# Two transformer blocks on one core: moving the second round of transposes behind the next scores on TensorE, in the attention of the first three layers

## What is computed

```python
def diff_attn(q, k, v, lam):
    s = jnp.einsum("bqhmd,bkhmd->bhmqk", q.astype(F32), k.astype(F32)) * (B_QK_DIM ** -0.5)
    p = jax.nn.softmax(s, axis=-1)
    a = p[:, :, 0] - lam * p[:, :, 1]
    return jnp.einsum("bhqk,bkhd->bqhd", a, v.astype(F32))
```

## Time and profile before

| | us |
|---|---|
| median of 3 runs | 4227.97 |
| lowest, highest | 4216.44, 4235.77 |
| the profiled execution | 4224.61 |
| its span, first to last instruction | 4222.8 |
| PE busy in it | 3709.6 (88%) |
| DVE busy | 1952.1 (46%) |
| ACT busy | 1164.9 (28%) |
| POOL busy | 401.1 (9%) |

### The profile page before, as it was taken

One profiled execution on the slowest core, in us unless ns is written; L12 is line 12 of the kernel. 1 busy time (PEld: TensorE's weight loads), 2 busy tenths in 40 slices (PEclk: granted clock), 3 DMA queues, 4 the chain that ended last, 5 costly groups with the idle time before them and its releaser, 6 DMA issues.

```text
span 4222.8 us, 50333 instructions
## 1 busy us (share of the span) xinstructions
PE 3709.6 (88%) x20543; PEld 2948.4 (70%) x20543; DVE 1952.1 (46%) x2990; ACT 1164.9 (28%) x1891; POOL 401.1 (9%) x340
## 2 busy tenths in 40 slices
PE   6987789999989778999898888899999679978996
PEld 4865577888878636777786546688888556657885
DVE  3443654424445364434322774542343544455454
ACT  3221422212222232222222552221121234433221
POOL 1030410000000031000000470000000013200000
PEclk8985999999999778999998999899999789989998
DMA  5430013323322101545411011232342111112331
GB/s 175 150 99 1 1 47 110 113 73 111 103 66 70 30 1 46 160 129 166 125 55 43 1 27 51 78 112 75 110 119 67 43 32 27 36 45 75 93 101 61
DMA packets 520933, 319.63 MB, mean 76 GB/s; under 512 B 51216, under 2 KB 512798, under 8 KB 520704
## 3 DMA queue, kind: packets, MB, share of 16 engines
q1 hardware_dynamic: 512160, 299.93, 24.5%
q0 software_dynamic: 8544, 16.47, 1.4%
HBM read 309.79 MB, written 4.55 MB: 74 GB/s over the span
## 4 chain that ended last, share of the span: by engine, by line
PE 83%; DVE 10%; ACT 4%; issue 3%; POOL 1%; DMA 0%; DVEq 0%; ACTq 0%; POOLq 0%
PE PS L878 79%; PE PS L1072 2%; DVE TMP L1782 1%; DVE HL L1765 1%; DVE ATT L1850 1%; DVE TMP L1718 1%; DVE TMP L1774 1%; DVE X L1725 1%; DVE X L2220 1%; ACT BIG L1456 1%; ACT SPH L1324 1%; DVE X L2223 0%; ACT TMP L1456 0%; DVE TMP L1799 0%; ACT TMP L1395 0%
## 5 line engine op out<-in xcount | busy, mean ns | idle before, releaser
L878 PE MATMUL PS<-HH,SPH 128*128 128x512 f32 (+1 forms) x3424 | 1193.7, 361 | 98.1 <-DVE HL L1765 68.8
L878 PE MATMUL PS<-HL,SPH 128*128 128x512 f32 (+1 forms) x3424 | 1167.0, 355 | 0.0
L878 PEld LDWEIGHTS PS<-HH,SPH 128*128 128x128 f32 x3424 | 654.6, 191 | 235.3 <-issue 78.9
L878 PE MATMUL PS<-HH,SPL 128*128 128x512 f32 (+1 forms) x3424 | 736.8, 353 | 0.0
L878 PEld LDWEIGHTS PS<-HL,SPH 128*128 128x128 f32 x3424 | 655.5, 191 | 88.4
L1701 DVE TENSOR_TENSOR SPL<-RAW,SPH 128x1024 fp32r<-128x1024 f32 (+2 forms) x367 | 458.8, 1250 | 536.6 <-ACT SPH L1324 536.5
L878 PEld LDWEIGHTS PS<-HH,SPL 128*128 128x128 f32 x3424 | 580.4, 190 | 91.1
L1324 ACT ACTIVATE SPH<-RAW 128x1024 fp32r<-128x1024 f32 (+2 forms) x367 | 393.1, 1071 | 575.9 <-PE PS L878 482.3
L878 PE MATMUL PS<-MH,SPH 128*128 128x512 f32 (+1 forms) x1056 | 367.1, 361 | 18.1 <-DVE ML L2272 18.1
L878 PE MATMUL PS<-ML,SPH 128*128 128x512 f32 (+1 forms) x1056 | 364.5, 360 | 0.0
L1943 DVE SCALAR_TENSOR_TENSOR X<-PS,MOD,X 128x512 f32<-128x512 f32 (+1 forms) x144 | 95.3, 662 | 524.5 <-PE PS L878 522.8
(11 more groups left out here) (305 smaller groups left out, 3879.0 us busy)
## 6 DMA issues: line engine op xcount, KB each, us to landing
MS<-in_l_w_ada SPq DMA_DIRECT2D x96, 512.0 KB, 3.7
RAW<-in_l_w_up SPq DMA_DIRECT2D x88, 512.0 KB, 4.2
MS<-in_w_mod SPq DMA_DIRECT2D x80, 512.0 KB, 3.7
RAW<-in_w_gate SPq DMA_DIRECT2D x44, 512.0 KB, 4.9
RAW<-in_w_val SPq DMA_DIRECT2D x44, 512.0 KB, 4.9
RAW<-in_w_down SPq DMA_DIRECT2D x32, 704.0 KB, 4.6
RAW<-in_l_w_down SPq DMA_DIRECT2D x32, 704.0 KB, 4.6
RAW<-in_w_in SPq DMA_DIRECT2D x40, 512.0 KB, 5.1
```

Source lines behind the costliest of these rows:

```text
L878: return pe.matmul(o, a, b, start=start, stop=stop)
```

## The change

In PE's program of the attention, only one round of a step (instead of two) is issued in front of the next step's scores, in the three layers that aren't MLA; the second one comes right behind the scores, in front of those that stood there before. The programs of ACT, DVE, Pool and SP are the same as before, as is everything in the fourth layer.

```diff
                 for n in range(A.n):
                     rr = A.rounds[n]
-                    for r in rr[:2]:
+                    ahead = 2 if A.mla else 1
+                    for r in rr[:ahead]:
                         step(r)
                     if n in A.tiles:
                         x = A.tiles[n]
...
                         for part in range(2):
                             scores(n + 1, part)
                     if not A.mla:
-                        for r in rr[2:]:
+                        for r in rr[1:]:
                             step(r)
```

## The result

The changed kernel takes **4270.8 us** (median of 6 runs, 4267.8 to 4274.6), the kernel before in the same comparison 4219.8 (6 runs, 4216.0 to 4235.8): ratio 1.0116, with an interval of 1.0098 to 1.0134. The forecast was 4270 with a range of 4240 to 4308, and the sign was as forecast. The difference, though, is 49 us by the ratio (41 to 57), and I had forecast 42.5 on a median of before (4228.0, three runs) that was some 8 us high.

A forecast was written before the change was run, and what follows sets the result against it. The prediction took the attention steps as bound by a ring of PE's scores, DVE's maxima and ACT's exponentials; +28.5 us for the longer ring and +14 for the clock made +42.5, forecast 4270 us, range 4240 to 4308.

The forecast's parts named there:

- The ring through ACT: First layer, step without output round: scores, round 1, ACT's read and second exponential in series, 4.44 us against 3.75.
- An output round that moves: First layer, step whose output round o (product with V) moves behind the scores: 6.85 us against 4.70.
- Rounds 0, 1 and o: First layer, step with two transpose rounds and an output round: o starts 0.33 us later, 6.29 us against 5.96.
- Layer 1: First attention: sixteen steps have both rounds and scores to exchange, together +12.4 us.
- Layer 2: Second attention: steps with and without output round alternate, 10.73 us a pair against 9.67; twelve steps, +6.4 us.
- Layer 3, plain: Third layer, plain attention: ten steps 55.2 us against 50.6, net of late scores regained; eighteen steps, +8.4 us.
- Neighbourhood: Third layer, neighbourhood attention: ten steps 59.2 us against 58.55, most loss won back; about nineteen steps, +1.3 us (-5 to +8).
- The clock: First three layers: PE's idle pieces of about 2.0 us drop its clock to 1.2 GHz; seven falls taken, +14 us.
- Rival (a): Clock swings: in most of PE's 24 gaps it comes back at 1.2 GHz, +74 us, 4302 us; chance 0.13.
- Rival (c): DVE or Pool sets most third-layer steps, no loss there and no clock fall: +14 us, 4242 us; chance 0.17.
- Rival (b): Early scores win in the third layer if ACT's second exponential is outside the ring: -17 us, 4211 us; chance 0.04.
- Rival (d): The exchange does nothing, since transposes were never next to late scores: 4228 us; chance 0.04.

The follow-up runs named there:

- e1: Changed kernel, but ACT reads round 1 behind its second exponential outside the fourth layer: 4226.6 us, ratio to the kernel before 1.0016.
- e9: Changed kernel plus PE filler: round 0's transposes done once more beforehand as identity matmuls, except behind output rounds: 4253.8 us, ratio to before 1.0080.
- e10: Changed kernel plus PE filler: three more passes of true transposes before round 0's, except behind output rounds: 4257.2 us, ratio to before 1.0085.
- e4: PE's new order in the third layer only, the rest as in the kernel before: 4239.5 us, ratio to before 1.0054.
- e6: Changed kernel plus PE filler: three passes of identity matmuls in front of round 0's transposes in every step: 4336.7 us, ratio to before 1.0272.
- e3: PE's new order in the first two layers (differential attention) only, the rest as in the kernel before: 4255.1 us, ratio to before 1.0081.
- e7: Kernel before with PE's new order in the third layer only and ACT's round 1 read behind its second exponential in three layers: 4221.8 us, ratio 0.9994.

## Why the prediction was right, step by step

- **The ring through ACT** (4.44 for 3.75): 4.47 measured, and e1 shows that ACT's order makes it. Right in mechanism and size.
- **An output round that moves** (6.85 for 4.70): 6.68. The steps without o behind it, short o and context: 4.31 and 4.53 for 4.23 and 4.44.
- **Rounds 0, 1 and o** (6.29): 6.08 without a fall of the clock (layer 2, below), so the term was 0.2 too dear; I let o start 0.33 later than it has to, while it follows the three transposes directly. With a fall, 7.72 (458.65 to 466.37).
- **A head** (26.25 without the clock): 27.71, with one fall in it, and 26.08 in e9, where none lies in it. **Layer 1**: +12.4 for the ring, and +17.7 measured. The sixteen steps without falls, put together from the changed kernel, e9 and e10, are 11.7 us longer than before; the other 6 go with the clock: four falls for two before, and a stage that began with some 20 us at 0.50 where before had 10 (clock record).
- **Layer 2** (10.73 for a pair of steps, 9.67 before): 10.55, first exponentials of ACT's timeline two steps apart:

```profile
1575.30 0.89 ACT L1457 ACTIVATE TMP<-PS,ATT 128x768 f32<-128x768 f32 x1
...
1579.77 0.90 ACT L1457 ACTIVATE BIG<-PS,ATT 128x768 f32<-128x768 f32 x1
...
1585.85 0.89 ACT L1457 ACTIVATE BIG<-PS,ATT 128x768 f32<-128x768 f32 x1
```

The twelve steps without falls are 5.8 us longer than before, for +6.4. The stage grew by 5.5: its granted clock was 0.90 against 0.87, for it has three falls for one but began with less time at the low level (by the clock record some 9 us at 0.50 outside of its falls, before some 20).
- **Layer 3, plain** (55.2 for ten steps, 50.6 before): 57.80. One fall at 2382.1 lies in them, 1.6; e4, which has this order in the third layer and no fall in these steps, takes 56.2, so the sum was 1.0 too small. Most of that lies in the four steps with a full output round (6.36 to 6.40 for the 6.2 of the prediction, and 7.18 for its 7.0). **Neighbourhood** (59.2 for ten, 58.55 before): 62.88. Two falls lie in it; e9 without any takes 59.7, so the 59.2 was 0.5 too small. But the 58.55 that I held against it has two falls in it as well, at 2428.4 and 2442.0 (the rows with the low clock). So the +0.65 for ten steps compares steps without falls with steps that have two; with two on both sides it is +4.3. This term, which I trusted least, failed: the falls of before count as won back in it, and they came again elsewhere in the stage, five for five. The third stage grew by 17.0 us where the two terms had 9.7, and not by time at the low clock, of which it has less than before (20.4 us for 27.3). First and last exponentials of the changed kernel, of e4 (plain steps) and of e9 (neighbourhood steps):

```profile
2374.96 0.90 ACT L1457 ACTIVATE HHF<-PS,ATT 128x768 f32<-128x768 f32 x1
...
2432.76 0.90 ACT L1457 ACTIVATE TMP<-PS,ATT 128x768 f32<-128x768 f32 x1
...
2463.09 0.71 ACT L1454 ACTIVATE BIG<-BIG,ATT 128x512 f32<-128x512 f32 x1
...
2525.97 0.71 ACT L1454 ACTIVATE TMP<-TMP,ATT 128x512 f32<-128x512 f32 x1
```

```profile
2358.27 0.90 ACT L1457 ACTIVATE HHF<-PS,ATT 128x768 f32<-128x768 f32 x1
...
2414.48 0.90 ACT L1457 ACTIVATE TMP<-PS,ATT 128x768 f32<-128x768 f32 x1
```

```profile
2456.91 0.71 ACT L1460 ACTIVATE BIG<-BIG,ATT 128x512 f32<-128x512 f32 x1
...
2516.62 0.71 ACT L1460 ACTIVATE TMP<-TMP,ATT 128x512 f32<-128x512 f32 x1
```

- **The clock** (+14: seven more falls at 1.9). That falls come with PE's idle pieces held (e6, e9, e10); a fall's price was somewhat too high (1.4 to 1.6), and the size of the term far too high. The changed kernel falls twelve times in its stages, but the kernel before already fell eight times there, and the head that I read had none. Four more falls are some 6 us, and the time at 0.50 in the stages grew by only 2.9 us in all (71.3 to 74.2), since two of the stages began with less of it. So the 13 us that e9 and e10 gain are not what the change costs by the clock: the kernel before has falls of its own to lose.
- **The sum** (28.5 for the ring, 14 for the clock; 40.2 us measured in the stages). By steps without falls the ring is 11.7 us in the first layer and 5.8 in the second, and in the third, which spent less time at 0.50 than before, at least about its 17.0: some 34 in all. That leaves 6 us or less for the clock. So the ring was priced some 6 too low, by the third layer's two terms (9.7 for 17.0; the other two layers were 0.7 and 0.6 too high), and the clock at least 8 too high. That the two add up to within 3 us of the measured 40.2 is luck.
- **Not every gap is followed by a fall**, as I had taken it: one fall to a head of five steps in layer 1. That an output round brings the clock back, as I had it, no run shows; in the first attention of the kernel before it came back at 421.3, and from the start of that stage PE had done nothing but scores until then. Rival (a) and the Trainium skill's rule of the swinging clock ("TensorE: Matmul & The Clock Gate", "A second HAM failure mode: psum-queue depth-cycling") describe what happens, in the kernel before as well, but (a) put a new fall on each of 24 gaps, and four came.
- **Rival (c)**, DVE absorbs it: no. The third layer grew by 17.0. **Rival (b)**, early scores win: not in the changed kernel, and its condition was named correctly: with ACT's second exponential out of the ring (e1) the third layer is 5.5 us shorter than before, a third of the 17 that I gave it. But these 5.5 us are falls of the clock that e1 doesn't have (none behind the first steps, five before); its plain steps are longer than before (52.2 us for ten, 50.6 before). Early scores do shorten the step in which they had waited 2.68 us: 6.63 us in the changed kernel, 7.44 in e3 with the old order and no fall there, 9.04 before with one. **Rival (d)**, no effect: no.
- **The step that was missing**: that the untouched stretches can change too. Of the 45.8 us in the span 5.6 lie there, and I had no term for them.

## What to carry to other kernels

Before work is moved on one queue, read the consumer's queue: what stands behind the read that will now wait? If it is something that others need (here a second exponential), the move turns slack into a chain, and the reader has to be moved with the work. Price such a move by walking once round the ring with rows of the timeline; here that gave the steps of the first two layers to 0.2 us. Look whether the rows on the side of before hold falls of the clock, and count falls on both sides or on neither: here one term of 0.65 us for ten steps was 4.3 for that reason. And a gain of some 10 us in 4200 in a stage is no gain of the kernel before the whole has been timed.

## What the runs showed of the hardware that I had not expected

**Untouched work changes its time with the clock.** Between the first attention and the second stand the same 5240 matmuls in all kernels. The stretch in before, after, e4 and e7, in this order, from the windows of each:

```profile
512.07:1513.59 1001.52, 917.81 (x5240) 766.81 (x5240) 433.71 (x603) 218.75 (x272) 16.38 (x32) 0.93 0.26 76
```

```profile
524.21:1532.85 1008.64, 923.32 (x5240) 772.52 (x5240) 433.54 (x603) 218.73 (x272) 16.37 (x32) 0.92 0.26 76
```

```profile
512.25:1524.77 1012.52, 927.40 (x5240) 775.12 (x5240) 433.61 (x603) 218.74 (x272) 16.38 (x32) 0.92 0.26 75
```

```profile
504.81:1504.71 999.90, 914.95 (x5240) 763.68 (x5240) 433.72 (x603) 218.74 (x272) 16.38 (x32) 0.93 0.26 76
```

DVE, ACT and POOL are busy for the same time to 0.2 us in each; PE is not, and the length goes from 999.9 to 1012.5. By the clock record of the traces e7 spends 143.5 us of it at 0.50, before 146.7, after 157.7 and e4 170.7. A microsecond at half the clock costs half a microsecond: 27.2 more of them in e4 than in e7 make 13.6 us, and 12.6 were measured. So the length goes with the time at the low clock. Why it is low for longer in one kernel than in another I did not find out: the stretch starts at another time in each, and from another state of the clock, and no run separates the two. Over the profiles of the ten experiments all that is not in the three stages took 3801 to 3820 us; it was 3807.5 before and 3813.1 after. This spread is larger than the 6 us of e7's gain. But e7's one profile is a short one (span 4210.4 for a median of 4221.8), and in it the rest of the kernel is 6 us shorter than before, not longer; so that its missing gain went there is argued, not shown.

**Transposes keep the clock up as matmuls do.** In e10 only transposes were added, and the falls went from twelve to three and the stages from 455.6 to 442.6; matmuls in e9 gave 442.3. These are float32 transposes that stand among float32 matmuls; no run has transposes alone. The Trainium skill, "TensorE: Matmul & The Clock Gate", "Part 4: PE-mode transpose", says that transposes don't count as PE's activity in the same way and that full speed doesn't set in for them. By that rule e10 would have been no faster than the changed kernel, 4271 us, with whatever of the filler shows on top; it took 4257, so here the runs speak against the rule. The falls carry this, for the times of the whole kernel alone are not clear of each other.

**A float32 product costs two transposes.** 0.24 us for 128x128 by 128x128 in a row of nine (e6), 0.11 to 0.12 for a transpose of that size (four in 0.60 to 0.66 us, the first with its start).
